# A layer pair in float32: later exponentials on ScalarE, and another order of the side lanes

## What is computed

```python
proj = h @ w_in[l]                      # 2048 x 5456: d_q d_k d_v s_q s_k s_v i_q i_k i_w
# differential attention, 8 heads, two maps of 64 dims each, values of 128
p1, p2 = softmax(mask(q1 k1^T)), softmax(mask(q2 k2^T))
diff_out = rms_norm((p1 - lam * p2) @ v, g_diff_sub) * (1 - lam_init)
# indexed sparse attention, 8 heads of 128, one shared k and v
score = sum_h relu(iq_h . ik) * iw_h    # 16 index heads; the top 64 keys of a query stay
dsa_out = softmax(s_q s_k^T where selected) @ s_v
mixed = concatenate([diff_out, dsa_out]) @ w_o[l]
x = x + gate_a * rms_norm(mixed, g_attn_post)
```

## Time and profile before

| | |
|---|---|
| median of 3 runs | 2428.31 us (2427.94 to 2430.77) |
| profiled execution | 2428.22 us, span 2426.9 us |
| PE busy | 2291.2 us (94%) |
| DVE busy | 1399.5 us (58%) |
| ACT busy | 1062.3 us (44%) |
| mean granted PE clock | 0.978 |

### The profile page before, as it was taken

How to read it: one execution, slowest core, us unless ns; L and a number is a source line. 1 busy time by engine, 2 the same in 40 slices (tenths; PEclk the granted TensorE clock), 3 DMA queues, 4 the chain that set the end, 5 groups by cost and what they waited for, 6 DMA issues and landing times.

```text
span 2426.9 us, 26309 instructions
## 1 busy us (share of the span) xinstructions
PE 2291.2 (94%) x10768; PEld 1861.1 (77%) x10768; DVE 1399.5 (58%) x1903; ACT 1062.3 (44%) x1469; POOL 0.7 (0%) x5
## 2 busy tenths in 40 slices
PE   4898989798999999999999999999999999999998
PEld 2676667676878888888887878788888888888886
DVE  1459898686666464454555555454544554554554
ACT  2333534444434444444444555555444444444443
POOL 0000000000000000000000000000000000000000
PEclk7999999899999999999999999999999999999999
DMA  7888678484776575556554644444555556556553
GB/s 296 333 314 306 216 262 285 153 306 166 247 273 243 192 259 191 191 191 191 191 189 143 210 157 154 153 152 152 185 196 192 188 184 197 183 186 194 187 190 139
DMA packets 255455, 505.69 MB, mean 208 GB/s; under 512 B 9077, under 2 KB 19662, under 8 KB 254182
## 3 DMA queue, kind: packets, MB, share of 16 engines
q1 hardware_dynamic: 255334, 504.00, 61.6%
HBM read 499.77 MB, written 4.19 MB: 208 GB/s over the span
## 4 chain that ended last, share of the span: by engine, by line
PE 82%; DVE 10%; ACT 3%; DMA 3%; issue 2%; SPq 0%; DVEq 0%; ACTq 0%
PE bank L566 26%; PE bank L568 25%; PE bank L567 25%; DVE wlo L1643 3%; DVE acc L1626 2%; PE bank L582 2%; DMA raw<-in_w_in_dram 2%; ACT whi L1033 1%; PE bank L650 1%; DMA raw<-in_w_ada_dram 1%; PE bank L520 1%; PE bank L590 1%; DVE x L1695 0%; ACT Ex_b L1162 0%; PE bank L673 0%
## 5 line engine op out<-in xcount | busy, mean ns | idle before, releaser
L1643 DVE TENSOR_TENSOR wlo<-raw,whi 128x1024 fp32r<-128x1024 f32 (+2 forms) x760 | 910.5, 1205 | 887.6 <-ACT whi L1033 887.1
L1033 ACT ACTIVATE whi<-raw 128x1024 fp32r<-128x1024 f32 (+2 forms) x760 | 790.1, 1044 | 1035.2 <-PE bank L568 949.1
L566 PE MATMUL bank<-whi,Ahi 128*128 128x512 f32 (+2 forms) x2304 | 912.5, 396 | 37.8 <-DVE wlo L1643 21.2
L567 PE MATMUL bank<-wlo,Ahi 128*128 128x512 f32 (+2 forms) x2304 | 897.0, 389 | 0.0
L568 PE MATMUL bank<-whi,Alo 128*128 128x512 f32 (+2 forms) x2304 | 896.6, 389 | 0.0
L566 PEld LDWEIGHTS bank<-whi,Ahi 128*128 128x128 f32 x2304 | 438.1, 190 | 141.1 <-DVE wlo L1643 31.3
L568 PEld LDWEIGHTS bank<-whi,Alo 128*128 128x128 f32 x2304 | 437.7, 190 | 90.3
L567 PEld LDWEIGHTS bank<-wlo,Ahi 128*128 128x128 f32 x2304 | 438.5, 190 | 83.2
L1626 DVE SCALAR_TENSOR_TENSOR acc<-raw,cs,acc 128x512 f32<-128x512 f32 x224 | 153.4, 746 | 0.0
L566 PE MATMUL bank<-whi,Fhi 128*128 128x512 f32 x352 | 137.7, 391 | 0.0
L568 PE MATMUL bank<-whi,Flo 128*128 128x512 f32 x352 | 137.0, 389 | 0.0
(11 more groups left out here) (291 smaller groups left out, 1345.2 us busy)
## 6 DMA issues: line engine op xcount, KB each, us to landing
raw<-in_w_in_dram SPq DMA_DIRECT2D x156, 1024.0 KB, 5.0
raw<-in_w_ada_dram SPq DMA_DIRECT2D x96, 1024.0 KB, 5.3
raw<-in_w_gate_dram SPq DMA_DIRECT2D x44, 1024.0 KB, 5.1
raw<-in_w_up_dram SPq DMA_DIRECT2D x44, 1024.0 KB, 5.1
raw<-in_w_down_dram SPq DMA_DIRECT2D x44, 1024.0 KB, 5.0
raw<-in_w_o_dram SPq DMA_DIRECT2D x16, 1024.0 KB, 5.2
raw<-in_w_o_mla_dram SPq DMA_DIRECT2D x16, 1024.0 KB, 4.9
raw<-in_w_o_conv_dram SPq DMA_DIRECT2D x16, 1024.0 KB, 4.9
```

The costliest lines, as they stand in the source:

```text
L566: pe.matmul(o, a_hi, w_hi, start=beg, stop=False)
L567: pe.matmul(o, a_hi, w_lo, start=False, stop=False)
L1033: act.activation(m.whi[:, i % NHL, :, 0:n], m.raw[:, c % NRAW, 2 * h:2 * h + 2, 0:n], ACT.Copy).then_inc(m.s_hi, 1)
L1643: dve.tensor_tensor(m.wlo[:, i % NHL, :, 0:n], m.raw[:, c % NRAW, 2 * h:2 * h + 2, 0:n], m.whi[:, i % NHL, :, 0:n].bitcast(F32), ALU.subtr ...
```

## The change

`exps` in `attention` (first block only) isn't issued at its step on ACT but noted down with `later`. `catch_up` issues what is noted, in order: in `chunk` right behind `split_to` of the next unit, and otherwise at the beginning of the next `tick`. So in a stretch with units ACT's order becomes: high part, exps, steps. Between chunks of two products, ACT's evacuation of a product's banks now also stands ahead of the exps noted down in its last tick. In `tick` lane 1 takes its step first, then lane 0, then lane 2, on all engines. What `mla_pair` calls is as before.

```diff
@@ Walk.__init__
+        self.late = []
@@ Walk.chunk
             self.split_to(UNIT_AT[LIN[min(self.unit + AHEAD, len(LIN) - 1)]])
+            self.catch_up()
             if mult:
                 mult(self.unit, h)
@@
+    def later(self, f, *args):
+
+        self.late.append((f, args))
+
+    def catch_up(self):
+        for f, args in self.late:
+            f(*args)
+        self.late = []
+
     def tick(self):
+        self.catch_up()
         if not self.lanes[1] and self.idle and self.can_take():
             self.lanes[1].append(self.idle())
-        for jobs in self.lanes:
+        for jobs in (self.lanes[1], self.lanes[0], self.lanes[2]):
             if jobs:
@@ scalar_program, attention
             k.use(b0), k.use(b1)
             yield
-            exps(ln, n % 2, scale)
+            k.later(exps, ln, n % 2, scale)
             yield
```

## The result

The changed kernel took 2413.95 us (median of four runs, 2411.88 to 2416.17) beside 2428.12 us for the kernel before: a ratio of 0.994 (95% interval [0.9928, 0.9953]), 14.2 us less. Run again later, the same program gave 2412.6 us beside 2428.99: 0.9934 [0.9922, 0.9947], 16.4 us less. The forecast was 2414.5. The added lines of the diff shift the numbers: L1033 is L1046 now, L1162 is L1175, L1643 is L1656, L663 is L676, L590 is L603, L2030 is L2043 and L2045 is L2058.

What follows compares the result with a forecast made beforehand. PE is busy for 94% of the span, so gains must come from its gaps in the attention stage (about 180 to 500 us). 5.9 + 1.1 + 1.35 + 4.5 + 1.5 - 0.5 = 13.85 us gives 2414.5 us, range 2406 to 2424.

Steps and rivals of the forecast that it cites:

- First, third and fourth item: PE gaps at 243.17, 293.88 and 323.68 us: 1.3, 1.07 and 3.5 us saved, together 5.9 at 324.
- Lane b at 400: Low part starts 1.7 us earlier, DVE leaves the combine 1.1 earlier, ahead of the modT wait: 1.1 us, bounds 0 and 2.7.
- Rope, combine: At 437.21 us lane a's rope goes behind lane b's combine on DVE: 1.35 us saved.
- The tail: PE's 6.45 us gap at 474.70: square root passes lane a's exps, 4.5 us saved, plus 1.5 of slow clock behind it.
- The new waits at turns: PE's turns wait for late exps, 0.1 to 0.2 us at three items: cost 0.5 us, bounds 0 and 3.2.
- The table loads: Two more ACT table loads of 1.28 us each, both where ACT waits for PE, so no cost in the sum.
- stretches after 500 us stay as they are: Sign in the profile after: stretches behind the attention stage unchanged but for the shift.
- 1: Rival: saved waits come back as waits for low parts, only 5.9 to 9 us left, 2419 to 2423; 0.20 together with 5.
- 2: Rival: slower, late exps hold PE at its turns, 2434 to 2446 us; chance 0.10.
- 3: Rival: all the gaps close, with the slow clock behind them, 20 to 25 us saved, 2403 to 2408; chance 0.10.
- 4: Rival: table loads reach the path in the tail and take 2.6 us of the gain, 2417 us; chance 0.05.
- 5: Rival: the deferral does nothing, only the order acts, 8.2 us saved, 2420 us; 0.20 together with 1.

Runs made afterwards that it cites:

- Experiments 2, 3 and 6: In this order: `defer_only`, `until_only`, and the changed kernel with the old lane order in ticks without a unit (2412.77 us).
- experiment 6: Changed kernel with the old lane order (0, 1, 2) in the ticks that run without a unit: 2412.77 us, ratio 0.9936 to the kernel before.
- `before_slow_exps`: Kernel before with three waited-for 128x128 copies on ACT ahead of each exps call of lanes a and b: 2439.52 us, ratio 1.0048.
- `order_only`: Changed kernel with exps issued at once, so the new lane order without the deferral: 2427.27 us, ratio 0.9995 to the kernel before.
- `defer_only`: Changed kernel with the lanes in the old order, so the deferral alone: 2417.27 us, ratio 0.9956 to the kernel before.
- `until_only`: Kernel before with the new lane order only in ticks that run without units, exps at once: 2425.05 us, ratio 0.9988.
- experiment 7: Three waited-for ACT copies ahead of each exps call of lanes a and b: kernel before 2439.52 us (`before_slow_exps`), changed kernel 2421.17 us.

## Why the prediction was right, point by point

**The time** (2414.5 against 2413.95 and 2412.6) and the side were right. Of its terms, by the first profile:

*First, third and fourth item: 5.9 predicted, 5.77 measured.* The first gave 1.16 (1.3 predicted). PE itself lost it again: 0.07 are left at 283.43, behind the turns that waited 0.21 and 0.37 us for exponentials. It was DVE that carried it on, through high parts that came earlier with PE:

```profile
275.54 1.22 DVE L1656 TENSOR_TENSOR wlo<-raw,whi 128x1024 fp32r<-128x1024 f32 x1 [2.06 <-ACT whi L1046]
```

This low part is 1.4 us nearer to the start of the stage than in before (280.03 there). At the third item the wait of 4.10 is gone and came back as low parts, 2.59 at 297.25 and 2.08 at 306.62, as said; the ledger stands at 2.1 there. The fourth item gave the other 3.7 (3.5 predicted). Its wait, put at 4 to 6 us, was 3.54, and 5.16 in the second profile, with the transposes at the same distance (133.67 and 133.64): in the first profile the matmuls behind the 2.08 us gap ran slower (1.28 us for three of them against 0.68, from 308.76 on), and the next wait was shorter by what that cost. DVE sets the time there, and PE's slack hides PE's own clock.

*Lane b at 400: 1.1 predicted, nothing gained from 324 to 418.* At the modT wait the ledger stands at 5.8, where it stood at the fourth item, not at 7.0. PE's wait is 0.8 us shorter there only because PE comes 0.8 later to it, by waits that the sum did not have (0.88 for a low part at 329.13, 0.36 for Ex_a at 340.86, 0.71 at 348.19). What PE waits for is DVE, and the step that failed is DVE's. The prediction named as a sign that DVE's 2.74 us ahead of this low part would be gone; 1.68 of them stayed:

```profile
393.53 1.23 DVE L1656 TENSOR_TENSOR wlo<-raw,whi 128x1024 fp32r<-128x1024 f32 x1 [1.68 <-ACT whi L1046]
395.20 0.18 DVE L1889 RECIPROCAL sm_b<-sm_b 128x4 f32<-128x4 f32 x1 [0.45 <-ACT Ex_b L1175]
```

DVE saved 1.06 us of idling and paid 0.45 at the combine, 0.6 in all, and it had lost 0.5 on the way there; a wait of 0.81 for one of PE's products at 337.44 is new.

*Rope, combine: 1.35 predicted, 1.35 measured.* From the unit at 428.21 to lane b's transposes (437.21) the ledger goes from 6.48 to 7.83. With the order alone it goes from -7.06 to -5.71, the same 1.35, and with the deferral alone from 6.45 to 6.46, nothing: the order does it, as predicted. In all the ledger gains 2.4 us from the modT wait to the unit at 441 (5.8 to 8.2), and the other 1.0 was in no term. It comes from matmuls that no longer run at the lower level of the clock. Behind the modT wait they give 0.7 (0.6 in the second profile). The matmuls behind lane b's transposes give 1.0 (turns 0.21 us apart before, 0.11 after), of which a longer wait for DVE's `Alo` takes 0.7 back (1.50 to 2.33 us). The deferral alone has the 0.7 and the 1.0 too, without the longer wait (1.67 us), and so comes to 1.7 in this stretch.

*The tail: 4.5 plus 1.5 of slow clock predicted, 7.9 measured* (8.2 to 16.1 in the ledger). PE's wait for the normalized heads is gone altogether: the unit that it held up starts at 456.97 instead of 474.70, which is 6.4 us more than was gained up to 441. The rest, 1.5, is the unit behind, no longer slow, as predicted; the granted clock of 414:475 is 0.92 against 0.83. The mechanism was the one told (square root ahead of lane a's exponentials), but its size was put too low: the prediction took 4.5 of the wait of 6.45, and all of it went. And the order was not the only cause. Experiments 2, 3 and 6 show that the deferral moves those exponentials by itself (3.4 us in the old order, and 5.2 in the changed kernel with the old order in the tail), that the new order there adds 2.7 to that, and that the order without any deferral gains 4.2 in this stretch, or 1.9 where only the ticks without a unit have it.

*The new waits at turns: 0.5 predicted, 2.2 measured* (1.6 in three for Ex_a, 0.6 in two for Ex_b), of which 0.84 and 0.37 lie in the tail. The estimate took one lane's exponentials in a row; in the tail lane b's and lane a's follow each other, which the prediction had in its upper bound (3.2) only. These waits are inside the figures above, not on top of them.

*The table loads: nothing predicted, nothing seen.* The two new ones are at 456.04 (L1175) and 495.97 (L1081) in the first profile. The activation behind a load starts 1.29 to 1.30 us after it in the four cases shown (the earlier trace rows and experiment 6); the 1.34 us idle ahead of the exponentials at 459.82 ended with DVE's maxima, not with the load. The Trainium skill ("ScalarE: Activation LUTs", What ACT_TABLE_LOAD costs) puts a switch with its drain at 2.66 us; these rows show no drain behind the load. The tail gained although its exponentials went behind the square root, against that page's rule (Table sets) to do all of one set first.

*The slow clock elsewhere: not in the sum.* From the diag wait on nothing in the code has changed. Yet this part lasts 1857.5 us in the profile of before and 1861.05 and 1859.85 in the two of after. Behind the same 10.32 us wait for diag, PE's timeline in the first profile of after:

```profile
556.45 0.76 PE L579 MATMUL bank<-whi,Ahi 128*128 128x512 f32 x1 [0.82 <-issue]
557.01 0.63 PE L580 MATMUL bank<-wlo,Ahi 128*128 128x512 f32 x1
557.43 0.63 PE L581 MATMUL bank<-whi,Alo 128*128 128x512 f32 x1
557.86 0.63 PE L579 MATMUL bank<-whi,Ahi 128*128 128x512 f32 x1
```

and in the second:

```profile
556.04 0.47 PE L579 MATMUL bank<-whi,Ahi 128*128 128x512 f32 x1 [0.82 <-issue]
556.35 0.40 PE L580 MATMUL bank<-wlo,Ahi 128*128 128x512 f32 x1
556.59 0.40 PE L581 MATMUL bank<-whi,Alo 128*128 128x512 f32 x1
556.82 0.40 PE L579 MATMUL bank<-whi,Ahi 128*128 128x512 f32 x1
```

The matmuls start 0.43 us apart in the one and 0.23 in the other, the two levels of the clock (1.2 and 2.4 GHz), though the work and the wait ahead of them were the same. The first profile loses 1.6 us here, and another 1.6 ahead of it, behind the wait of 1.90 us at 470.36 (16.1 to 14.5 in the ledger). Each of the two loses about 1.6 behind the wait for gt, which is 2.05 and 1.98 us long there against 1.61 in before, where the matmuls stay fast. What comes late there is a DMA: DVE, which PE waits for, itself waits 5.00 and 4.93 us for the load of G, against 4.55 in before. Of fourteen profiles the wait for gt is 1.89 to 2.22 us in five, with the lower level of the clock behind each, and 1.50 to 1.73 in nine, with the upper level. In fourteen profiles this last part is 1857.1 to 1857.8 us in five (before, `before_slow_exps`, `order_only`, `defer_only`, `until_only`) and 1858.8 to 1861.1 in nine. Each part of the change alone is in the first group. But all nine of the second have both parts, the new order in the ticks with units and at least one lane's exponentials put behind, and none of the five has. So this loss may be a cost of the combination and not chance; no run decides it. It gave back 2.4 to 3.6 of the 14.5 to 16 us that the stage won in these profiles. The prediction's sign that stretches after 500 us stay as they are did not hold.

**So the side and most mechanisms were right, but that the time came within 2 us is partly luck:** the sum was 1.2 too much up to the modT wait (the term at 400), 1.0 and 1.9 too little in the two parts behind, and it left out 2.4 to 3.6 us of slow matmuls behind the stage, which take back about what the others add. **Of the rivals,** 1 held only in its first half (the third item's wait did come back; the fourth's and the later ones' did not, and only lane b's at 400 us brought nothing). 2 did not decide the result, but experiment 7 prices it at 0.73 us for each microsecond that the exponentials are late (7.8 of 10.7). 3 did not happen; its argument against itself, DVE's load at 300:324, held (23.2 of 24 us now). 4 did not happen. 5 was wrong as a whole: its gains at the rope and in the tail are there, but up to the modT wait the order alone loses 6.4 us, since it puts a waiting instruction ahead of a ready one on ACT.

## What to carry to other kernels

On an engine whose queue is in order, an instruction that waits for another engine has the price of everything queued behind it: look in the timeline of the engine that waits (here ACT, 13.8 us ahead of one group of exponentials), and read what stands behind, not what it waits for itself. Counted from the kernel with the new order alone, moving it behind the ready work of the same step gave two thirds of the gain here (10 of about 15 us), and moving it once more, behind the next unit's first instruction, the rest. The limit is where its own reader begins to wait. And the effects of two edits need not add: changing the order of the lanes was worth nothing with the waiting instruction in its old place, and some 3 to 5 us with it out of the way.

## What the runs showed that I had not expected

- A row's start in two profiles of the same code differs: the matmul ahead of the touched stage starts between 179.95 and 184.24 us in fourteen profiles. Distances from a common row agree to 0.1 us between two profiles of the same kernel (133.67 and 133.64, 228.30 and 228.24), up to a place where slow matmuls enter.
- The same wait of 10.32 us is followed by matmuls at the upper level of the clock in some profiles and at the lower in others; a wait of 1.61 us was followed by the upper level, one of 1.98 by the lower. So over all places the length of a gap does not alone say which level follows, though at the wait for gt it sorted all fourteen profiles.
- Three copies of 0.31 us, which delay an exponential by 0.89 us, cost the kernel before 0.93 us each time by the medians (11.2 in twelve) and 1.05 by the ledger (12.6 behind the tail, and 14.2 at the diag wait, with 1.6 us of slow matmuls between). On the average nothing covered an exponential there.
